# One of an attention's four exponent differences is moved from VectorE to GpSimd, from the second level on

## The reference

```python
b = jnp.cumsum(gi.astype(jnp.float32), axis=-2)          # gi = log f
rel = b[..., :, None, :] - b[..., None, :, :]
decay = jnp.exp(jnp.where(lower, rel, -jnp.inf))
attn = jnp.sum((qi[..., :, None, :] * ki[..., None, :, :]) * decay, axis=-1)
o_intra = jnp.einsum('bhts,bhsv->bhtv', attn, vi)
```

## Time and profile before

| | |
|---|---|
| median of 3 runs | 2401.29 us (2400.64 to 2411.91) |
| the profiled execution's own time | 2412.53 us |
| its span | 2410.8 us |
| granted TensorE clock, mean | 0.982 |
| busy: TensorE, VectorE, ScalarE, GpSimd | 95%, 73%, 51%, 12% |
| the stage at hand | 517.6 to 577.4 us of the span |

### The profile page before, as it was taken

One profiled execution on the slowest core, in us unless ns is written; L12 is line 12 of the kernel. 1 busy time (PEld: TensorE's weight loads), 2 busy tenths in 40 slices (PEclk: granted clock), 3 DMA queues, 4 the chain that ended last, 5 costly groups with the idle time before them and its releaser, 6 DMA issues. The chain is left out here.

```text
span 2410.8 us, 46354 instructions
## 1 busy us (share of the span) xinstructions
PE 2285.9 (95%) x15836; PEld 1989.3 (83%) x15836; DVE 1764.9 (73%) x3166; ACT 1234.5 (51%) x1973; POOL 295.1 (12%) x285
## 2 busy tenths in 40 slices
PE   7989989977999999999999998899999999999998
PEld 7657657863899999997888878589999999888886
DVE  6765775775568878886767778666887888777776
ACT  5444544565344465554555453744446555445544
POOL 0000000000000000003444320000000000433442
PEclk9999999999999999999999999999999999999999
DMA  7555555765447776667777775245776666777775
GB/s 223 186 210 136 194 201 180 290 232 209 156 145 229 228 217 197 186 189 222 241 240 241 241 249 176 105 158 165 228 227 210 201 189 187 233 241 242 240 241 176
DMA packets 247734, 497.92 MB, mean 207 GB/s; under 512 B 58040, under 2 KB 134072, under 8 KB 244304
## 3 DMA queue, kind: packets, MB, share of 16 engines
q1 hardware_dynamic: 247632, 496.55, 64.7%
HBM read 461.82 MB, written 34.65 MB: 206 GB/s over the span
## 5 line engine op out<-in xcount | busy, mean ns | idle before, releaser
L2762 PE MATMUL psum<-split_operands 128*128 128x512 f32 x3072 | 701.7, 391 | 9.4 <-DVE split_operands L2750 9.4
L2762 PEld LDWEIGHTS psum<-split_operands 128*128 128x128 f32 x3072 | 579.9, 189 | 130.7 <-issue 10.2
L2494 PE MATMUL psum<-split_operands 128*128 128x256 f32 x4096 | 543.5, 286 | 8.9 <-ACT split_operands L2528 8.8
L2494 PEld LDWEIGHTS psum<-split_operands 128*128 128x128 f32 x4096 | 510.5, 192 | 10.4 <-ACT split_operands L2528 10.4
L2717 POOL TENSOR_TENSOR arena<-arena,residual_gates 128x256 f32 (+1 forms) x256 | 281.1, 1099 | 1723.4 <-POOLq L114 1319.8
L2753 DVE TENSOR_TENSOR split_operands<-weights_ring,split_operands 128x1024 fp32r<-128x1024 f32 x256 | 316.7, 1237 | 203.5 <-ACT split_operands L2733 203.5
L2733 ACT CAST split_operands<-weights_ring 128x1024 fp32r<-128x1024 f32 x256 | 269.5, 1053 | 352.9 <-PE psum L2762 349.4
L2571 DVE TENSOR_TENSOR split_operands<-weights_ring,split_operands 128x1024 fp32r<-128x1024 f32 x256 | 313.2, 1224 | 103.0 <-ACT split_operands L2528 102.2
L346 PE MATMUL psum<-split_operands 128*128 128x256 f32 x2496 | 306.8, 284 | 7.5 <-DVE split_operands L362 6.5
L346 PEld LDWEIGHTS psum<-split_operands 128*128 128x128 f32 x2496 | 301.3, 192 | 15.1 <-DVE split_operands L362 8.5
L2498 PE MATMUL psum<-split_operands 128*128 128x256 f32 x2048 | 288.9, 284 | 0.0
(11 more groups left out here) (320 smaller groups left out, 2000.4 us busy)
## 6 DMA issues: line engine op xcount, KB each, us to landing
weights_ring<-in_peer_u_dram SPq DMA_DIRECT2D x256, 512.0 KB, 3.6
weights_ring<-in_peer_v_dram SPq DMA_DIRECT2D x256, 512.0 KB, 4.3
expert_activations<-residual_gates SPq DMA_DIRECT2D x256, 128.0 KB, 1.9
residual_gates<-expert_activations SPq DMA_DIRECT2D x256, 128.0 KB, 4.0
split_words<-in_w_ada_dram SPq DMA_DIRECT2D x20, 768.0 KB, 6.2
weights_ring<-in_w_in_dram SPq DMA_DIRECT2D x6, 2048.0 KB, 9.2
weights_ring<-in_hg_w_in_dram SPq DMA_DIRECT2D x5, 2048.0 KB, 8.3
arena<-in_hg_w_in_dram SPq DMA_DIRECT2D x5, 2048.0 KB, 7.9
```

The costliest lines, as they stand in the source:

```text
L2494: nc.tensor.matmul(K.ps[:, 4 + b, 0:SEQ], u_t[:, b, 0, k], h[:, wh, k], start=(k == 0 and wh == 0), stop=False)
L2762: return K.nc.tensor.matmul(K.ps[:, 4 + 2 * t + half], g[:, s, w, t * P:(t + 1) * P], vs[:, s % 2, wv, half * 512:(half + 1) * 512], start ...
```

## The change

The difference i = 2 of the units n = 1, 2, 4, 5, 6, 7 is made by GpSimd in a queue of its own, with the semaphore `exps_pool`. ScalarE's exponential of the queries' half waits for it too, and so does SyncE's load of the second half of the output weights.

```diff
+POOL_LEVELS = [n for n in range(1, len(UNITS)) if UNITS[n] != CROSS]
...
-def level_exponent(K, H, pair, L, i):
+def level_exponent(K, H, pair, L, i, engine=None):
...
-    return K.nc.vector.tensor_tensor(out, a, b, op)
+    return (engine or K.nc.vector).tensor_tensor(out, a, b, op)
...
+        exps_pool = sem("exps_pool")
...
+        @block.gpsimd
+        def _(pool):
+            for n in POOL_LEVELS:
+                if n >= BUFS:
+                    pool.wait_ge(scored, n - BUFS + 1)
+                level_exponent(K, H, kq[:, n % BUFS], UNITS[n], 2, nc.gpsimd).then_inc(exps_pool, 1)
...
                 level_exponent(K, H, kq[:, n % BUFS], L, 1).then_inc(exps_k, 1)
-                level_exponent(K, H, kq[:, n % BUFS], L, 2)
                 level_exponent(K, H, kq[:, n % BUFS], L, 3).then_inc(exps_q, 1)
...
             for half, exps in enumerate((exps_k, exps_q)):
+                if half == 1:
+                    sp.wait_ge(exps_pool, len(POOL_LEVELS))
                 sp.wait_ge(exps, NU - 1)
...
                 if n >= 1:
                     act.wait_ge(exps_q, n)
+                if n in POOL_LEVELS:
+                    act.wait_ge(exps_pool, POOL_LEVELS.index(n) + 1)
```

## The result

The changed kernel is slower by 0.26%: the ratio to the kernel before is 1.0026, 95% interval 1.0019 to 1.0033, with medians of 2412.69 and 2407.01 us over 22 runs each. One of the 22 of the kernel before, at 3259.96 us, counts as slow and has no part in the ratio. That is 5.7 us by the medians and 4.6 to 7.9 us by the interval. The forecast was +4.9 us, 2406.2 us against the 2401.29 us of the first three runs. The kernel before has now a higher median than then, within the spread that those three showed.

What follows compares the result with a forecast made beforehand. VectorE's queue up to `factors(7)`, then TensorE's tail, was taken to set the stage's time. Terms +2.46, -1.14 and +3.54 us gave 4.86, so 2401.29 + 4.9 = 2406.2 us, range 2397 to 2418.

Steps and rivals of the forecast that it cites:

- what would make it wrong: In TensorE's tail, gaps of 2.93 and 2.35 us run at their own pace and swallow VectorE's lateness, or grow.
- The hold: VectorE and GpSimd instructions reading two SBUF operands exclude each other; the second stands still, VectorE for 2.02 us per difference.
- h: Time VectorE is held by one GpSimd difference: 2.02 us, bounds 0 and 2.96; total 6h - 7.26 us, break-even 1.21 us.
- up to `factors(0)`: Start of VectorE's queue in the stage: three differences and two GpSimd turns, 7.45 us in place of 4.99, +2.46 us.
- unit 2: In VectorE's queue, this unit's moved difference is gone: -1.14 us.
- units 4 to 7: In VectorE's queue, each unit costs +2.02 - 1.135 = +0.885 us, together +3.54 us.
- The tail: TensorE's last 9.5 us or so of the stage, after `factors(7)`; claimed untouched by the change.
- Each takes its turn once: Each GpSimd difference gets in once between VectorE's closely queued instructions and holds VectorE for h.
- rival D: GpSimd gets its turn only when VectorE idles, and ScalarE waits for it: +14 us, 2415.3 us; chance 0.10.
- one sign of the profile after: In the attention stage's profile after, ScalarE would show no wait for GpSimd.
- B: The strided views interleave or nothing is held on VectorE: -5.7 us, 2395.6 us; chance 0.10.
- C: GpSimd is slow on these views, h above 3.21 us: loss over 12 us, +16.7 us at h = 4; chance 0.10.

Runs made afterwards that it cites:

- `drop`: The changed kernel with the six differences left out; GpSimd only raises the semaphore and ScalarE's exponential has scale 0; ratio to the kernel before 0.9996.
- `write_only`: The changed kernel with GpSimd storing zeros by memset in place of its six differences; ratio to the kernel before 1.0002.
- `ask_later`: The changed kernel with GpSimd also waiting for `exps_k` from unit 4 on; VectorE's queue 50.61 us, stage 62.38 us.
- `release`: The changed kernel with a small VectorE memset added after the crossing unit's two differences; ratio to the kernel before 1.0025.
- `double`: VectorE keeps all 24 differences and GpSimd makes six more into a spare place, edited from the changed kernel; ratio to the kernel before 1.0046.
- `ahead`: The kernel before, without GpSimd differences, with VectorE making unit 1's four differences at the end of the stage before; ratio to the kernel before 0.9990.

## Why the prediction was right

**What bounds the stage.** VectorE's queue, as said, for a loss. The queue's lengths add up: -5.67 us where only the gain was left (5 x 1.135 = 5.675), and +9.58 where only the hold was, where 10.4 was expected, or 9.7 with one turn beside a copy from PSUM. For a gain the statement was too strong: TensorE's late instructions and its clock are close behind, and take back a large part of what VectorE wins (of 5.67 us at least 1.8 by the interval of `drop`, and at least 3.3 by that of `write_only`). The prediction named this as what would make it wrong; here it didn't, since VectorE's queue became longer and not shorter.

**The hold.** The mechanism was right and h was a little too large: 2.02 us forecast, 1.77 us measured. `factors(0)` starts 6.94 us after the first difference, which is 3 x 1.135 + 2 h. The extrapolation from 768 to 1024 elements was the step that was off: a straight line from 0.57 us at 256 to 1.77 us at 1024 gives 1.37 us at 768, where the prediction read 1.54; why is not shown. The Trainium skill, "GPSIMD Engine Reference", section "Elementwise — side-by-side cycle accounting", gives 4497 ns for 2048 elements. The estimate of h from it, 2.25 us, is further off.

**The sum.** Term by term: up to `factors(0)` +2.46 forecast, +1.95 measured; unit 2 -1.14 and -1.14 (three differences in 3.41 us); units 4 to 7 +3.54 and +1.95, of which 4 x (1.77 - 1.135) = 2.54 less the 0.6 us beside the copy from PSUM. The queue: +4.86 forecast, +2.76 measured. With the measured h the forecast's own formula gives 3.4 us, and 2.8 us less the 0.6. The tail, forecast at nothing, came to +1.07 in this pair of profiles; its scatter is 1.6 us in the kernel before, and `ask_later` and `release`, with nearly the changed kernel's queue, have tails of 11.77 and 14.72. So the sign and the mechanism were right, but it is in part luck that the total came so near (+4.9 forecast, +5.7 measured): the queue's share was 2.1 us too large, and some 3 us that the time shows beyond it were forecast at nothing.

**The turns.** "Each takes its turn once" was right for the sum. That GpSimd gets the next boundary held for five of six; rival D, starving, was there for unit 4 alone. With it one sign of the profile after failed, that ScalarE doesn't wait for GpSimd. It cost little, since ScalarE's exponential, late until 540.10, was over at 542.01, and `factors(4)` started at 546.85, behind VectorE's own held differences.

**The rivals.** B (nothing is held): against it stand 7.01 us for three differences, and `double`. Its price of -5.7 us was wrong besides: `drop` gives VectorE the gain that B says and takes 0.04% less time, from 0.16% less to 0.08% more. C (h over 3.21 us): h is 1.77 us, and GpSimd takes 1.92 us on the strided views when it has its turn at once.

**What stays open.** The stage accounts for 3.8 us in the first pair of profiles, and 2.2 us against the second one of before, where the runs say 4.6 to 7.9. From the start of the span to the stage, where the change touches no code, the twelve profiles with that part unchanged differ by up to 6.7 us (the stage starts at 512.53 to 519.25). Single profiles can't place a remainder of 1 to 4 us, and no run here did.

## What to carry to other kernels

Before work goes from a full VectorE to an idle GpSimd, look for a place in the trace where both read SBUF at once, and take the time for which VectorE is held as the price. Here it was 1.77 us of hold for 1.135 us of work, so each instruction moved was a loss, though GpSimd was idle and nearly never late. And of a queue that is full to the brim, ask what comes right behind it before a gain is booked in full: here a gain of 5.7 us in VectorE's queue left no measurable one in the time.

## What the runs showed of the hardware that was not expected

- After the crossing unit's two instructions GpSimd was kept out over four boundaries of VectorE's queue or more (its instruction took 9.56 to 10.77 us in four profiles), until VectorE copied from PSUM; with a memset of two elements behind them it got the next boundary (4.15 us, one profile).
- TensorE stood up to 4.54 us (in `ahead`) at places 128 products apart, and went on 2.3 to 2.6 us after a 16 KB packet of instructions had started. That it waits for these is inferred. It stood 2.35 us even at a DMA share of 0.07.
- With its steps moved out of the tail TensorE began the next stage at a mean granted clock of 0.68 and not 1.00: 24 products in 7.84 us where they took 5.42.
